# Two transformer blocks on one core: the modulation tiles, the row tiles and the first norm put in another order

## The reference, cut to what matters

```
mod = (c @ w_ada + b_ada)                     # w_ada: 1024 x 6144
sh_m, sc_m, gt_m, sh_f, sc_f, gt_f = jnp.split(mod, 6, axis=-1)
h = rms_norm(x, g_pre_mix) * (1.0 + sc_m) + sh_m
z = h @ w_in                                  # then u, f, q, k, v
```

## Time and profile before

| | |
|---|---|
| median of three runs | 3256.84 us (3255.87 to 3257.34) |
| the profiled execution | 3251.52 us |
| its span, first to last instruction | 3249.7 us |
| TensorE busy | 3108.7 us (96%) |
| VectorE busy | 2162.2 us (67%) |
| GpSimd busy | 1696.7 us (52%) |
| ScalarE busy | 1417.7 us (44%) |
| mean granted TensorE clock | 0.985 |

### The profile page before, as it was taken

How to read it: one execution, slowest core, us unless ns; L and a number is a source line. 1 busy time by engine, 2 the same in 40 slices (tenths; PEclk the granted TensorE clock), 3 DMA queues, 4 the chain that set the end, 5 groups by cost and what they waited for, 6 DMA issues and landing times.

```text
span 3249.7 us, 41580 instructions
## 1 busy us (share of the span) xinstructions
PE 3108.7 (96%) x15015; PEld 2551.1 (79%) x15015; DVE 2162.2 (67%) x3025; ACT 1417.7 (44%) x2717; POOL 1696.7 (52%) x1248
## 2 busy tenths in 40 slices
PE   7988899899999999999999999989999999999998
PEld 4875587678887888788887878878987888887876
DVE  6779662899997133866668781168836866667854
ACT  4147462655553123443434551058724443334543
POOL 3310347666556767645545552344367545545563
PEclk9989999999999999999999999999999999999999
DMA  5534435422423543243336344546442343345443
GB/s 204 127 126 129 132 77 181 144 86 78 129 85 117 196 153 104 85 136 104 98 134 213 110 146 137 182 126 161 115 181 66 115 135 104 98 162 185 141 145 130
DMA packets 338054, 428.48 MB, mean 132 GB/s; under 512 B 62167, under 2 KB 234394, under 8 KB 337092
## 3 DMA queue, kind: packets, MB, share of 16 engines
q1 hardware_dynamic: 261368, 259.81, 27.3%
q10 hardware_dynamic: 71532, 148.90, 12.4%
q0 software_dynamic: 4960, 17.22, 1.7%
HBM read 321.12 MB, written 111.05 MB: 133 GB/s over the span
## 4 chain that ended last, share of the span: by engine, by line
PE 78%; DVE 9%; issue 4%; POOL 3%; ACT 3%; DMA 2%; SPq 1%; ACTq 0%; POOLq 0%; DVEq 0%
PE PS L970 69%; PE PS L2940 3%; PE PS L2957 1%; PE PS L2924 1%; PE PS L897 1%; POOL w_lo L297 1%; DVE pt L826 1%; POOL dg_ab L3116 1%; DMA w_raw<-w_out 0%; DVE dwl L1880 0%; DVE px L834 0%; PE PS L2588 0%; DVE ss L1320 0%; DMA wr12a<-ffn_w_down 0%; DVE h_lo L964 0%
## 5 line engine op out<-in xcount | busy, mean ns | idle before, releaser
L1341 POOL TENSOR_TENSOR sl<-ss,sh 128x512 fp32r<-128x512 f32 x300 | 451.9, 1513 | 510.0 <-ACT sh L1332 510.0
L297 POOL TENSOR_TENSOR w_lo<-w_raw,w_hi 128x512 fp32r<-128x512 f32 (+1 forms) x284 | 402.2, 1447 | 9.4
L1624 DVE TENSOR_TENSOR cset<-cset,PS 128x512 f32<-128x512 f32 x354 | 231.8, 682 | 250.7 <-PE PS L970 250.4
L970 PE MATMUL PS<-h_hi,sh 128*128 128x512 f32 x960 | 373.7, 389 | 0.6 <-issue 0.3
L970 PE MATMUL PS<-h_lo,sh 128*128 128x512 f32 x960 | 373.5, 389 | 0.0
L970 PE MATMUL PS<-h_hi,sl 128*128 128x512 f32 x960 | 373.5, 389 | 0.0
L293 POOL CAST w_hi<-w_raw 128x2048 fp32r<-128x2048 f32 x71 | 143.7, 2024 | 428.7 <-DMA w_raw<-w_in 161.1
L1332 ACT ACTIVATE sh<-ss 128x512 fp32r<-128x512 f32 x300 | 189.0, 631 | 340.1 <-DVE ss L1320 329.5
L1846 POOL TENSOR_TENSOR dal<-dar,dah 128x512 fp32r<-128x512 f32 x154 | 237.4, 1551 | 188.3 <-ACT dah L1840 185.8
L1320 DVE TENSOR_TENSOR ss<-sr 128x512 f32<-128x512 f32 x300 | 316.0, 1054 | 1.1 <-PE PS L970 1.1
L970 PE MATMUL PS<-x_hi,sh 128*128 128x512 f32 x720 | 281.7, 391 | 14.7 <-DVE x_lo L1312 7.1
(11 more groups left out here) (412 smaller groups left out, 7330.9 us busy)
## 6 DMA issues: line engine op xcount, KB each, us to landing
sr<-ffn_w_gu SPq DMA_DIRECT2D x80, 512.0 KB, 5.0
dar<-sd SPq DMA_DIRECT2D x154, 256.0 KB, 2.7
w_raw<-w_down SPq DMA_DIRECT2D x44, 512.0 KB, 4.3
sd<-st_odd ACTq DMA_DIRECT2D x22, 1024.0 KB, 4.5
xs<-px ACTq DMA_DIRECT2D x40, 512.0 KB, 2.9
sr<-w_up SPq DMA_DIRECT2D x40, 512.0 KB, 5.1
w_raw<-w_out SPq DMA_DIRECT2D x32, 512.0 KB, 4.6
w_raw<-w_in SPq DMA_DIRECT2D x28, 512.0 KB, 6.1
```

Of the source, the lines that this page charges most:

```text
L297: op = e.tensor_tensor(w_lo[b][:, s], w_raw[b][:, s], w_hi[b][:, s].bitcast(F32), ALU.subtract)
L970: mm = e.matmul(o, a[ai], b[bi], start=start and first, stop=stop and end, skip_group_check=shared)
L1341: e.tensor_tensor(s.lo[p][:], src, s.hi[p][:].bitcast(F32), ALU.subtract).then_inc(S("s_op"), 1)
L1624: e.tensor_tensor(out, out, PS[:, b, :], op).then_inc(S("s_ev"), 1)
```

## The change

The queue of SyncE is reordered: scale tiles k = 0 to 3, shift tiles k = 0 to 3, scale tiles k = 4 to 7, the first weight chunk, shift tiles k = 4 to 7, the second weight chunk, and only then the row pairs x1, x2, x3. ScalarE scales all four of the first row tiles, and it copies the scale row to `mod2`. TensorE does its two small jobs (`cd`/`wf` and `crow`) between scale tiles 3 and 4, turns the first three sets of rows before it turns the scale, and makes the shift last, to another bank. VectorE takes reciprocals of T = 0 and 1 ahead of the accumulator, those of T = 2 and 3 behind its second tile, makes `cc` behind its fourth, and adds b_ada to scale and shift in two operations.

```diff
             x_rows(0)
-            ada_rows(0, 8)
+            ada_rows(1, 0, 4)
+            ada_rows(0, 0, 4)
+            ada_rows(1, 4, 8)
+            stream_load(e, 0, 1)
+            ada_rows(0, 4, 8)
+            stream_load(e, 1, 2)
             x_rows(1)
-            stream_load(e, 0, 1)
-            ada_rows(8, 16)
-            stream_load(e, 1, 2)
             x_rows(2)
...
             for T in range(4):
                 norm_sq_act(e, 0, T)
-            for T in (0, 2):
-                norm_scale_act(e, 0, T)
+            for T in range(4):
+                norm_scale_act(e, 0, T, ("m_xn", "m_xd")[T % 2])
...
+            e.wait_ge(S("prep_mm"), ADA_MM)
+            e.activation(mod2[:], PSr[0:1, 3072:4096], ACT.Copy).then_inc(S("md2"), 1)
...
-        VC_T, ADA_MM, FF_W, C_T, MOD_MM, MD_T, GT_T, GR_T = range(1, 9)
+        VC_T, FF_W, C_T, ADA_MM, MD_T, MOD_MM, GT_T, GR_T = range(1, 9)
...
             for k in range(KT):
+                if k == 4:
+                    e.wait_ge(S("ff_ld"), 32)
...
             mm.then_inc(S("prep_mm"), 1)
-            e.wait_ge(S("acc0"), KT)
+            for q in range(3):
+                norm_set(e, 0, q)
             e.wait_ge(S("md2"), 1)
-            mod_pe(e, acc0, PS[:, 6, 0:8])
             for k in range(KT):
                 mm = e.transpose(PS[:, 6, 8 + k:9 + k], mod2[:, k * P:(k + 1) * P], ident[0:1, 0:1])
             mm.then_inc(S("prep_mm"), 1)
+            e.wait_ge(S("acc0"), KT)
+            mod_pe(e, acc0, PS[:, 7, 0:8])
...
+            for T in range(2):
+                norm_r_dve(e, 0, T)
             for k in range(KT):
+                if k == 2:
+                    for T in range(2, 4):
+                        norm_r_dve(e, 0, T)
+                if k == 4:
+                    e.wait_ge(S("prep_mm"), C_T)
+                    e.tensor_scalar(cc[:, 0, :], PS[:, 4, 0:SSM_W], sgn[:, 0:1], None, ALU.mult).then_inc(S("cc"), 1)
+                    e.tensor_scalar(cc[:, 1, :], PS[:, 5, 0:SSM_W], -1.0, None, ALU.mult).then_inc(S("cc"), 1)
                 if k % 2 == 0:
                     e.wait_ge(S(f"tile_ld0{k // 2}"), 32)
...
-            e.wait_ge(S("prep_mm"), ADA_MM)
-            e.tensor_copy(mod2[:], PSr[0:1, 3072:4096]).then_inc(S("md2"), 1)
-            norm0_rows_dve(e, 0)
...
+            e.tensor_tensor(mod[:, 8:16], PS[:, 6, 8:16], vec[:, VC["b_ada"] + 8:VC["b_ada"] + 16], ALU.add).then_inc(S("mod_v"), 1)
             e.wait_ge(S("mod_v"), 1)
             gain_pre_dve(e, 0, 1, "g_pre_mix")
+            e.wait_ge(S("prep_mm"), MOD_MM)
+            e.tensor_tensor(mod[:, 0:8], PS[:, 7, 0:8], vec[:, VC["b_ada"]:VC["b_ada"] + 8], ALU.add).then_inc(S("mod_v"), 1)
```

More of the change, by code:

```diff
@@ L354, in prep_sp, with ada_rows @@
             w = t["w_ada"][0].rearrange("(k p) n -> k p n", p=P)
-            def ada_rows(first, end):
-                for i in range(first, end):
-                    k, v = i // 2, 1 - i % 2
+            def ada_rows(v, first, end):
+                for k in range(first, end):
+                    i = 2 * k + 1 - v
                     e.dma_start(ada[i][:], w[k, :, v * D:(v + 1) * D]).then_inc(S(f"tile_ld{v}{k // 2}"), 16)
@@ L454, in prep_pe @@
             for k in range(KT):
+                if k == 4:
+                    e.wait_ge(S("ff_ld"), 32)
+                    for a in range(2):
+                        for c in range(2):
+                            mm = e.matmul(PS[:, 0, (a * 2 + c) * HD:(a * 2 + c + 1) * HD], cd[:, c, :], wf[:, a, :], start=True, stop=True)
+                    mm.then_inc(S("prep_mm"), 1)
+                    e.wait_ge(S("c_ld"), 64)
+                    for i in range(2):
+                        for m in range(3):
+                            mm = e.transpose(PS[:, 4 + i, m * P:(m + 1) * P], crow[i][:, m, :], ident[:])
+                    mm.then_inc(S("prep_mm"), 1)
                 if k % 2 == 0:
@@ L536, in prep_dve @@
                     e.scalar_tensor_tensor(acc0[:], ada[2 * k + 1][:], vcol("c", k), acc0[:], ALU.mult, ALU.add).then_inc(S("acc0"), 1)
-            e.wait_ge(S("prep_mm"), ADA_MM)
-            e.tensor_copy(mod2[:], PSr[0:1, 3072:4096]).then_inc(S("md2"), 1)
-            norm0_rows_dve(e, 0)
-            e.wait_ge(S("prep_mm"), C_T)
-            e.tensor_scalar(cc[:, 0, :], PS[:, 4, 0:SSM_W], sgn[:, 0:1], None, ALU.mult).then_inc(S("cc"), 1)
-            e.tensor_scalar(cc[:, 1, :], PS[:, 5, 0:SSM_W], -1.0, None, ALU.mult).then_inc(S("cc"), 1)
             e.wait_ge(S("prep_mm"), MD_T)
-            e.tensor_tensor(mod[:, 0:16], PS[:, 6, 0:16], vec[:, VC["b_ada"]:VC["b_ada"] + 16], ALU.add)\
-             .then_inc(S("mod_v"), 1)
+            e.tensor_tensor(mod[:, 8:16], PS[:, 6, 8:16], vec[:, VC["b_ada"] + 8:VC["b_ada"] + 16], ALU.add).then_inc(S("mod_v"), 1)
             e.wait_ge(S("mod_v"), 1)
             gain_pre_dve(e, 0, 1, "g_pre_mix")
+            e.wait_ge(S("prep_mm"), MOD_MM)
+            e.tensor_tensor(mod[:, 0:8], PS[:, 7, 0:8], vec[:, VC["b_ada"]:VC["b_ada"] + 8], ALU.add).then_inc(S("mod_v"), 1)
         def chain_exp_dve(e):
@@ L699, in gates_dve @@
                             r(vec[:, VC["b_ada"] + 16:VC["b_ada"] + 48]), ALU.add).then_inc(S("mod_v"), 1)
-            e.wait_ge(S("mod_v"), 2)
+            e.wait_ge(S("mod_v"), 3)
             gain_pre_dve(e, 1, 4, "g_pre_ffn")
@@ L860, in norm_r_dve, with norm_scale_act @@
             e.reciprocal(stat[:, 5, T:T + 1], stat[:, 4, T:T + 1]).then_inc(S("m_r"), 1)
-        def norm_scale_act(e, n, T):
+        def norm_scale_act(e, n, T, done="m_xn"):
             e.wait_ge(S("m_r"), n * 8 + T + 1)
-            e.activation(xrow(n, T), norm_row(n, T), ACT.Copy, scale=stat[:, 5, T:T + 1]).then_inc(S("m_xn"), 1)
+            e.activation(xrow(n, T), norm_row(n, T), ACT.Copy, scale=stat[:, 5, T:T + 1]).then_inc(S(done), 1)
         def norm_scale_dve(e, n, T):
@@ L900, in first_pe @@
         def first_pe(e, n, units):
-            if not half_ahead(n, 0):
+            if n and not half_ahead(n, 0):
                 for q in range(3):
@@ L939, in norm_out_act @@
                 e.wait_ge(S("gain"), 1)
+                e.wait_ge(S("mod_v"), 2)
             if n > 1 and hf == 0:
```

## The result

The changed kernel takes 3268.64 us (median of 8 runs, 3265.91 to 3270.61), the kernel before 3256.36 (8 runs, 3252.64 to 3257.88). The ratio is 1.0035, 95% interval 1.0026 to 1.0044, so it is slower by 11.4 us (8.5 to 14.3). Forecast were 8.8 us and a time of 3265.6, range 3260 to 3270. The measured time lies in that range. The direction, the place and the mechanism were right; two terms of the sum were too small.

The account below looks back on a forecast made before the run. TensorE, busy in 96% of the span, can lose time only where it stands still, as at the start. First `fold` 10.8 us later, less 2.0 regained, gave 8.8 on the 3256.84 median: 3265.6, range 3260 to 3270.

Parts of the forecast that it names:

- The queue: SyncE's loads: x1 lands at 38.6 instead of 22.2, last modulation tile at 32.9, second chunk at 36.0, third 46.6.
- ScalarE: ScalarE after x1 lands: last root at 41.45, four tiles scaled by 45.8, `bd` to 47.7, scale row copied by 49.0.
- VectorE's queue: Six accumulator steps behind T=3's reciprocal: 10.9 us, accumulator ready at 52.5, bounds 50.4 and 54.7.
- The shift's matmuls: TensorE's matmuls after the accumulator: 3.0 us, between 1.92 and 3.8, with the clock expected at 0.50.
- From F to the eighth product: Window from first `fold` to eighth tile's product: 11.6 us instead of 13.57, so 2.0 come back; bounds 11.6 to 13.6.
- F: ScalarE's first `fold`, at 45.12 before; forecast at 55.9, 10.8 later, between 52.6 and 59.9.
- The sum: Whole kernel: eighth product at 67.5, 8.8 us later, carried over to a median of 3265.6.
- A: Rival at SyncE's queue: x1 lands early, out of issue order; 3.6 us faster, 3253.2; chance 0.03.
- B: Rival at the start: small overlap with GpSimd and clock up; 5.5 to 6.5 us later, 3262.3 to 3263.3; chance 0.19.
- D: Rival behind the eighth product: a later wait takes up 3 to 9 us, 3257 to 3262; chance 0.07.
- C: Rival at the start: overlaps and clock cost in full; 11 to 15 us later, 3268 to 3271.6; chance 0.15.
- the likeliest case: The main forecast for the whole kernel: 8.8 us later, 3265.6, own range 3263.5 to 3268; chance 0.56.

Follow-up runs that it names:

- e5: Changed kernel with GpSimd's split of the second and third weight chunk held until the accumulator is complete; ratio 1.0033 against the kernel before.
- e1: Changed kernel with the load of x rows 2 and 3 moved back to sixth in MiB; ratio 1.0005 against the kernel before.
- e2: Changed kernel with VectorE's reciprocals of row tiles 2 and 3 moved behind the last accumulator step; ratio 1.0018 against the kernel before.
- e3: Kernel before with only the new order of loads, engines' order unchanged; ratio 1.0001 against the kernel before.
- e10: e2 with the shift's matmuls ahead of the turned rows on TensorE, to another bank; ratio 1.0016 against the kernel before.
- e4: Changed kernel with the old order of loads, so only the edits on the engines remain; ratio 0.9993 against the kernel before.
- e9: e7 with VectorE's small chain_first operations moved behind the subtractions of the second half of the rows; ratio 0.9983 against the kernel before.
- e7: Changed kernel with x1 sixth, first weight chunks behind all sixteen tiles, late reciprocals moved, six sets turned early; ratio 0.9982 against kernel before.

## Why the prediction was right, point by point

1. **The queue.** x1 at 38.6, by counting MiB: measured 38.55. The second chunk at 36.0: 36.09. The third at 46.6: 46.70.
2. **ScalarE.** Last root done at 41.45 (measured 41.39), rows scaled at 45.8 (45.55), copy's end at 49.0 (48.39; the copy took 1.01, under my bound of 1.1).
3. **VectorE's queue.** Right in kind: six steps behind the late reciprocal. The step that was mis-sized is "tile 2 2.0, tile 3 1.3, ... tiles 4 and 5 2.6, tiles 6 and 7 4.0", ready at 52.5: measured 54.5. I had three dear steps. There are four: 2.17, 2.80, 2.11 and 2.17 us in the chain after, and the first of the six, for which I had 2.0, took 1.41, though GpSimd was subtracting. The one of 2.80 (47.34) lies beside GpSimd's rounding of the third chunk, which I had taken for quiet; it took 2.36 there against 1.89 alone. e5 shows the whole as GpSimd's share: 54.5 against 50.4. My low bound (50.4) was the price without GpSimd to the tenth, and my high one (54.7) the nearest to what came.
4. **The shift's matmuls.** 3.0 forecast, 3.57 measured, at the clock of 1.2 GHz (table of stretches below). Five kernels have 3.55 to 3.58 (changed, e1, e2, e3, e10), six 1.95 (e4 to e9), and before 1.92; the upper bound, twice 1.92, was the nearer guess. My 3.0 was the price of neither level. I had TensorE idle from about 28; it worked on the scale to 32.4 and stood idle for 13.28 us before 45.70, and for 5.14 and not 3 us before the shift. That the clock was down there was right, but not certain: e5, after the same transposes, had it up.
5. **From F to the eighth product.** 11.6 forecast, 70.05 - 58.46 = 11.59 measured; 2.0 us came back as said. GpSimd's subtractions ended at 56.9, before F, so the steps were as cheap as I had taken them. (My terms, 7 x 1.34 + 1.45 + 0.7, add up to 11.5.)
6. **The sum.** 2.0 + 0.6 are the 2.6 by which F (58.46 for 55.9) and the shift (11.4 for 8.8) exceed the forecast.

Busy time by stretch after (columns as in rows 8):

```profile
40.00:45.00 5.00, 0.00 (x0) 0.00 (x0) 3.70 (x4) 4.97 (x8) 4.04 (x3) 0.50 1.04 380
45.00:50.00 5.00, 3.76 (x20) 3.35 (x20) 4.96 (x5) 3.19 (x10) 3.15 (x2) 0.50 0.16 51
50.00:55.00 5.00, 0.41 (x2) 0.41 (x3) 4.83 (x5) 0.00 (x0) 5.00 (x3) 0.50 0.00 0
55.00:60.00 5.00, 3.17 (x15) 3.08 (x15) 0.92 (x3) 1.54 (x3) 1.89 (x2) 0.50 0.00 0
```

**The rivals.** A (x1 early) did not occur. Its 3.6 us faster was too hopeful, because the four last shift tiles still stood together behind the first chunk: in e2, where the accumulator waits for no row and the queue is that of the change, it was ready at 39.1, not 36.9, and e1, the nearest run to A, gained nothing. B and D did not occur; nothing later took up any of it. C, 11 to 15 later by dear overlaps and a low clock, is what came: 11.4 lies at the lower end of its span and just above the forecast's own range. So the case with 0.15 held what the likeliest case missed, and the direction rested on both. From what the Trainium skill's page "SBUF — State Buffer", section "Who interferes with whom", says of an exclusive lock I had worked out 2.7 us a step and F near 58. (The Trainium skill's page states the block for a whole instruction of the two-port modes; of a VectorE instruction with two SBUF inputs it says that it contends.) The measured steps are 2.1 to 2.2 where pieces alternate, and 2.8 beside a rounding. That sum came nearer than mine by luck: three steps at 2.7 make nearly what four at 2.3 and a cheap first one made (ready at 54.6 by it, 54.5 measured).

**Open:** what decides whether the clock is up at the shift's matmuls; the late rows' own 3.9 us; and the profiled executions differ by 5.6 us more than the marks explain. As the changed kernel's own runs span 4.7 us and those before 5.2, I take it for scatter; it wasn't traced to a place.

## What to carry to other kernels

Engines work in order, so a short operation that waits for a late load holds everything behind it: before moving a load back in a queue, follow each of its users on every engine and ask what ready work stands behind the first wait. Two edits that are harmless alone can meet there (+0.9 and -2.1 gave +11.3), so measure the corners, not only the sum. Loads can be timed by counting the bytes ahead of them when the queue is full. Chunks whose split disturbs the engine on the path may be better loaded behind what that engine needs, as in e7; the split then disturbs whatever comes next (F to the eighth product: 15.5 us in e7, 11.6 in the changed kernel).

## What the runs showed of the hardware

- An accumulator step of VectorE (two SBUF inputs, 128x1024) takes 1.3 us alone and 2.13 (8.54 for four) beside GpSimd's subtractions; those take 1.23 a piece alone (4.92 for four, e5) and 1.97 beside it (7.87). One of each in turn takes about 2.1 us, more than either alone but less than their sum of 2.5. First GpSimd's timeline in e5, then VectorE's in the kernel e1:

```profile
29.99 4.92 POOL L297 TENSOR_TENSOR w_lo<-w_raw,w_hi 128x512 fp32r<-128x512 f32 x4
```

```profile
33.05 8.54 DVE L552 SCALAR_TENSOR_TENSOR acc<-ada,vec,acc 128x1024 f32<-128x1024 f32 x4 [4.14 <-DMA ada<-w_ada]
```

- GpSimd's rounding of a chunk, with one input, is slowed by VectorE too: 1.89 alone, 2.36 to 2.90 beside accumulator steps (changed kernel, e4).
- A VectorE operation with two SBUF inputs can be small and still pay: the gain (128x8) took 0.17 us with GpSimd idle (e5), and 0.27 (e2) to 1.72 (e7) with GpSimd at work.
- Sixteen small matmuls of the shift: 1.95 us at the full granted clock (2.4 GHz), 3.55 to 3.58 at half (1.2 GHz). The idle time right before them doesn't tell which: after 1.05 us they ran at the full clock (e5), after 5.14 (changed kernel), 5.66 (e10), 7.21 (e3) and 7.61 us (e1) at half, but in e2 at half too without any, since there the clock had not risen again after 13.21 us of idle time ahead of the turned rows.
- ScalarE copied one partition of 1024 columns from PSUM in 1.01 us; VectorE needed 1.21.
